# Cache pages laid four tokens to a partition, with evictions, page turns and key groups moved, in the sample loop of a decoder step

## The chip, the cores and the metric

The kernel runs as one program on one core of a Trainium2 chip. A core has five engines that follow their own instruction queues and meet through semaphores: PE (matmul and transpose), DVE (vector), ACT (scalar and activation), POOL and SP. In this kernel SP and POOL mostly issue DMAs, which the same 16 DMA engines carry out. The metric is device time of one execution, in microseconds (us), over three runs.

## The reference

One decoder layer is computed for a prompt of 256 tokens and a sample group of 8 sequences with 8 new tokens each. Every sample sequence has 1024 cached tokens, in 8 pages of 128 tokens that a page table names:

```
past = (gather_pages(cache_cmp_kv[l], page_table), gather_pages(cache_sel_kv[l], page_table), state_win_kv[l],
        gather_pages(cache_diff_k[l], page_table), gather_pages(cache_diff_v[l], page_table))
o_win  = local_attend(q_rot, win_all, pos, wpos)                    # last 512 tokens
o_cmp, p_cmp = compressed_attend(q_nsa, cmp_all, pos, ...)          # blocks of 32 tokens, stride 16
sel_idx = select_blocks(p_cmp, pos, tk)                             # 16 of 17 blocks of 64 tokens
o_sel  = selected_attend(q_rot, sel_all, sel_idx, pos)
o_nsa  = g0 * o_cmp + g1 * o_sel + g2 * o_win
o_diff = diff_attention(q_diff, k_all, v_all, pos, kpos, lam)       # softmax0 - lam * softmax1, then RMSNorm
x = x + (sig * (o_nsa @ w_br_nsa) + sig' * (o_diff @ w_br_diff)) @ w_out
x = x + moe_ffn(rmsnorm(x))                                         # top 4 of 32 experts
```

A softmax over cached keys and the sum over their values don't depend on the order in which the keys stand, so long as scores, masks and values have the same order. The change rests on this. The rows of the caches are 512 floats a token (difference keys, difference values) and 256 floats a token (selected, window and compressed K/V).

## The kernel before

The program runs in stages: input projection, prompt attention, the sample loop, the merge of the branches with the output projection, and the experts, whose weights (12 MB an expert, 32 experts and more blocks) stream in from the time at which the merge frees their places. The change is in the sample loop.

The loop handles two sequences a turn, in four turns; the last one is written out apart. All engines walk it in step, by counters. In a turn PE does this, in order:

- `dif_scores(0)`: the score products of the first sequence (L632) with the transposed keys `kdT`;
- 16 products of the compressed K hidden layer, `hidden(0, l)` (L587), with the transposes of the second sequence's key pages, groups `kd0` to `kd7` (L573), one after each odd `l`;
- `dif_scores(1)`, the compressed keys, 16 products `hidden(1, l)` with the groups `sel0` to `sel3`, `win0`, `win1` (cached keys transposed) and `pd0` to `pd2` (softmax weights transposed) between them;
- scores of the selected and window branch (L714 to L722), `dif_values(0)` and `dif_values(1)` (L648), then the groups `nk0`, `nk1` (key pages of the next turn's first sequence), `ps0`, `ps1`, `jo`, `pw`, `pm`, `nk2` to `nk5`;
- `nsa_values` (L662), `nk6`, `nk7` and `o` (both outputs transposed).

Each group of transposes goes to one of three PSUM banks in turn, so group n waits until group n-3 has been evicted. `LOOP_ENGINE` says whether ACT (L828) or DVE (L780 and on) evicts a group; each does its own in the order of its instruction list. A group of page keys is four 128x128 transposes of one page.

The buffers of the loop and who fills them:

- `dk_raw` (8 pages of keys, one set) by SP, `dk_pages` (L483): page by page, each as its group has been transposed. SP fills it twice a turn.
- `sel_raw`, `win_raw` by SP (L469, L474), after `nsa_values` of the turn before, in SP's order behind the key pages.
- `dv_raw` (values, two sets of 8 pages) by POOL, `values_in` (L510), after `dif_values`.
- `cmp_raw` (8 pages) by POOL, `cmp_pages` (L455), after DVE has turned the page before (STREAM_TRANSPOSE, `turn_pages`, L898). PE's `hidden(0, 0)` waits for all 16 turns of pages of its turn (`cmp_turned`).

At the top of a turn SP and POOL also read page numbers from the page table. A page stands with its 128 tokens on 128 partitions: one DMA of a key page writes 128 rows of 2 KB, one of a selected page 128 rows of 1 KB. The masks in the code follow that order: `oldw` for the first 8 window tokens, and the mask of the one dropped selection block (`dropm`, 14 candidates), which is added to columns 64 to 959 of the scores (L957).

After the loop, SP loads weights and stored gate values into freed places (`sync_merge`, helper line L251).

Of the kernel before, what the change touches and what calls it, by code (L numbers as in the profile page):

```python
# [17 lines left out]
ALU = mybir.AluOpType  # L18
# [4 lines left out]
D = 1024  # L23
# [7 lines left out]
NPAGE = PAST // PAGE  # L31
NPOOL = (5 * NB * NPAGE + 3) // 4
WIN = 512
# [24 lines left out]
def shape_constants():  # L58
# [27 lines left out]
    a["oldw"] = np.where(np.arange(NT)[None] > t[:, None], 0, NEG)  # L86
# [6 lines left out]
    a["blk"] = np.tile(np.arange(1, PAST // SB - 1), (128, 1))  # L93
# [54 lines left out]
def build(nc, io, const_a, at_a, const_b, at_b):  # L148
    ctx = ExitStack()
    with ctx:  # L150
# [16 lines left out]
        def bank(k, n=512, off=0):  # L167
# [6 lines left out]

        dv_raw = [[at(6144 + 512 * j, 512) for j in range(NPAGE)],
                  [at(34304 + 512 * j if j < NPAGE - 1 else 30720, 512) for j in range(NPAGE)]]
# [16 lines left out]
        winT, selT = at(31232, 2, WIN), at(32256, 2, PAST)  # L193
# [29 lines left out]
        pgs, mass, imp, dropm = alloc(NCC + 1), alloc(14, 4), alloc(14), alloc(14)  # L223
# [224 lines left out]

        def cmp_pages(eng, pages, i, b, these=range(NPAGE), first=False):
# [8 lines left out]
        def sync_attention(sp, early):  # L458
# [4 lines left out]
            def sel_pages(i, pages, first=False):  # L463
                if not first:
                    past(sp, l_pv, i * VALUES)
                for b in range(2):
                    for k in range(2):
                        for h in range(4):
                            sp.dma_start(sel_raw[:, b, 4 * k + h],  # L469
                                         sel_d[bass.ds(pages[b][4 * k + h], 1)].rearrange("a p n -> (a p) n")).then_inc(sel_in[2 * b + k], 16)  # L470

            def win_pages(i):
                for b in range(2):
                    sp.dma_start(win_raw[:, b], win_d[bass.ds(2 * i + b, 1)].rearrange("a (s p) n -> p (a s) n", p=128)).then_inc(win_in[b], 16)  # L474

            def dk_pages(i, b, pages, first=False):

                for pg, page in enumerate(pages):
                    if first and b:
                        past(sp, l_tp, pg + 1)  # L480
                    elif not first:
                        past(sp, l_tp, i * L_TP + (NPAGE - L_TP + group_at(f"nk{pg}" if b else f"kd{pg}") + 1))
                    sp.dma_start(dk_raw[:, pg], kd_d[bass.ds(page, 1)].rearrange("a p n -> (a p) n")).then_inc(dk_in[pg // 4], 16)  # L483
# [19 lines left out]
        def pool_attention(pool, st):  # L503
            vd_d = io["cache_diff_v"][0].rearrange("n p h e -> n p (h e)")

            def values_in(pages, i, b, first=False):
                for pg, page in enumerate(pages):
                    if pg == 0 and not first:
                        past(pool, l_pv, i * VALUES + ((PV_D1 if b else PV_D0) - VALUES))
                    pool.dma_start(dv_raw[b][pg], vd_d[bass.ds(page, 1)].rearrange("a p n -> (a p) n")).then_inc(dv_in[2 * b + pg // 4], 16)  # L510
# [49 lines left out]
        def pe_attention(pe):  # L560
# [30 lines left out]
            def turn(i, final):  # L591
# [49 lines left out]
                def dif_values(b):  # L641
                    for k in range(2):
                        pe.wait_ge(dv_in[2 * b + k], i * 64 + 64)
                    for j in range(NPAGE + 1):
                        for h in range(4):
                            out = pv_dif[b][32 * h:32 * h + 32]
                            if j < NPAGE:
                                nc.tensor.matmul(out, ptl[:, j, 32 * h:32 * h + 32], dv_raw[b][j][:, 128 * h:128 * h + 128], start=(j == 0), stop=False)  # L648
# [2006 lines left out]
```

## Time and profile before

| | us |
|---|---|
| runs of the kernel | 1458.56, 1460.26, 1460.40 (median 1460.26) |
| the profiled execution | 1461.19 |
| its span | 1459.5 |
| PE busy | 1389.9 (95%) |
| second and third turn of the loop (279.26 to 375.96) | 48.48 and 48.22 |

How to read it: the span is cut into stretches in which different things bind. Durations of single instructions are means over their group. "DMA share" is how much of the time of the 16 DMA engines the packets took; it can be over 1, since packets overlap. An instruction on PE can be idle for a wait while the engine's busy share still reads high. Landing times run from the issue of a DMA to its semaphore. Time that an engine waits matters only if it is the engine on which the others wait. The granted clock of TensorE was 0.993 over the span (the higher level, 2.4 GHz).

### The profile page before, as it was taken

The page shows a single profiled execution, that of the slowest core. Times are in us where ns is not written, and L with a number is a line of the kernel's source. Part 1 is how long each engine was busy: PE and PEld are TensorE (multiplying, and loading weights), DVE is VectorE, ACT ScalarE, POOL GpSimd, SP SyncE. Part 2 cuts the span into 40 slices and gives each one's busy share as a digit, 9 for nine tenths or more (in the row PEclk, how much of TensorE's full clock was granted, in tenths as well). Part 3 has the DMA queues.
Part 4 walks back from the last instruction along what each step waited for, and adds up shares of the span by engine and source line. Part 5 has one row for each costly group of instructions (what it writes and reads, how often), then busy time and mean ns, then how long its engine had stood idle before and what let it go on. Part 6 is the DMA issues. An engine that isn't in the chain of part 4 may idle for free.

```text
span 1459.5 us, 19997 instructions
## 1 busy us (share of the span) xinstructions
PE 1389.9 (95%) x7350; PEld 614.5 (42%) x7350; DVE 473.1 (32%) x1110; ACT 280.8 (19%) x584; POOL 106.1 (7%) x217
## 2 busy tenths in 40 slices
PE   7999998989999999999999999999999999999987
PEld 3446554766674454333333333333333333333322
DVE  1114474545633653132122221331331322213314
ACT  2003343444533121000101101101001001011002
POOL 1000223325400000000000000000000000000000
PEclk9999999999999999999999999999999999999999
DMA  7334686799988769999999999999999999999996
GB/s 264 115 115 169 245 174 219 192 302 279 300 261 241 298 252 428 427 428 430 427 428 430 428 428 428 429 428 428 428 429 427 428 430 427 428 430 428 428 427 256
DMA packets 92878, 509.45 MB, mean 349 GB/s; under 512 B 19066, under 2 KB 37986, under 8 KB 67586
## 3 DMA queue, kind: packets, MB, share of 16 engines
q1 hardware_dynamic: 77602, 480.99, 82.3%
q0 software_dynamic: 15232, 27.89, 6.6%
q8 instruction: 25, 0.41, 0.1%
q14 instruction: 19, 0.16, 0.0%
HBM read 502.25 MB, written 10.62 MB: 351 GB/s over the span
## 4 chain that ended last, share of the span: by engine, by line
PE 75%; DMA 19%; ACT 2%; issue 2%; SPq 1%; DVE 1%; ACTq 0%; DVEq 0%
PE PS L1435 25%; PE PS L1465 11%; DMA arena<-in_w_gate_up 10%; PE PS L1409 6%; PE PS L352 5%; DMA arena<-in_w_down 4%; PE PS L2129 4%; PE PS L1401 4%; PE PS L1116 2%; PE PS L1297 2%; DMA arena<-in_cache_sel_kv 2%; PE PS L587 2%; PE PS L573 2%; DMA arena<-in_cache_diff_k 2%; PE PS L361 1%
## 5 line engine op out<-in xcount | busy, mean ns | idle before, releaser
L1435 PE MATMUL PS<-arena 128*64 128x512 f32 x2048 | 456.2, 595 | 13.9 <-DMA arena<-in_w_gate_up 12.9
L1435 PEld LDWEIGHTS PS<-arena 128*64 128x64 f32 x2048 | 141.5, 137 | 295.2 <-issue 263.1
L1465 PE MATMUL PS<-arena 128*64 128x512 f32 x1024 | 226.9, 594 | 2.3 <-DMA arena<-in_w_down 2.2
L1891 DVE TENSOR_SCALAR arena<-PS 128x512 f32<-128x512 f32 x32 | 22.1, 692 | 451.1 <-PE PS L1444 450.1
L1465 PEld LDWEIGHTS PS<-arena 128*64 128x64 f32 x1024 | 71.8, 137 | 150.5 <-issue 144.3
L1409 PE MATMUL PS<-arena 128*128 128x512 f32 (+1 forms) x180 | 84.2, 608 | 0.0
L1401 PE MATMUL PS<-arena 128*128 128x512 f32 (+1 forms) x192 | 79.4, 617 | 4.5 <-ACT arena L1601 3.7
L1258 POOL COPY arena<-arena 96x64 bf16 (+1 forms) x34 | 8.1, 240 | 996.0 <-PE PS L1472 944.7
L352 PE MATMUL PS<-arena 128*128 128x512 f32 (+1 forms) x192 | 78.9, 572 | 1.6 <-DMA arena<-in_w_in 1.6
L573 PE MATMUL PS<-arena 128*128 128x128 f32 (+1 forms) x456 | 67.8, 281 | 12.1 <-DMA arena<-in_cache_diff_k 5.5
L1812 DVE TENSOR_TENSOR arena<-PS,arena 128x512 f32<-128x512 f32 x32 | 21.8, 688 | 163.7 <-PE PS L1417 161.2
L587 PE MATMUL PS<-arena 128*128 128x252 f32 x256 | 71.1, 392 | 3.8 <-DVE arena L898 3.8
L1586 ACT ACTIVATE arena<-arena 128x512 f32<-128x512 f32 x32 | 20.2, 630 | 269.7 <-DVE arena L1891 269.7
L1593 ACT ACTIVATE arena<-PS 128x512 f32<-128x512 f32 x32 | 19.1, 597 | 251.0 <-PE PS L1452 251.0
L573 PEld LDWEIGHTS PS<-arena 128*128 128x128 f32 (+1 forms) x456 | 53.6, 143 | 26.8 <-ACT arena L828 7.4
L1600 ACT ACTIVATE arena<-PS 64x512 f32<-64x512 f32 x31 | 18.3, 591 | 226.6 <-PE PS L1472 226.6
L2129 PE MATMUL PS<-arena 128*128 128x512 f32 x128 | 59.1, 603 | 0.6 <-ACT arena L2366 0.6
L828 ACT ACTIVATE arena<-PS 128x512 f32<-128x512 f32 (+2 forms) x75 | 40.9, 561 | 85.9 <-PE PS L573 78.8
L352 PEld LDWEIGHTS PS<-arena 128*128 128x128 f32 x192 | 37.0, 194 | 43.1 <-issue 41.6
L1409 PEld LDWEIGHTS PS<-arena 128*128 128x128 f32 (+1 forms) x180 | 31.6, 188 | 46.3 <-issue 46.3
L455 POOL DMA_DIRECT2D arena<-in_cache_cmp_kv x64 | 43.5, 687 | 79.2 <-DVE arena L898 78.9
L587 PEld LDWEIGHTS PS<-arena 128*128 128x128 f32 x256 | 43.8, 196 | 11.2 <-DVE arena L898 7.5
(293 smaller groups left out, 1279.4 us busy)
## 6 DMA issues: line engine op xcount, KB each, us to landing
arena<-in_w_gate_up SPq DMA_DIRECT2D x128, 2048.0 KB, 20.1
arena<-in_w_down SPq DMA_DIRECT2D x62, 2048.0 KB, 22.2
arena<-in_w_in SPq DMA_DIRECT2D x9, 2048.0 KB, 12.6
arena<-in_cache_diff_k SPq DMA_DIRECT2D x64, 256.0 KB, 6.8
arena<-in_cache_diff_v POOLq DMA_DIRECT2D x64, 256.0 KB, 8.7
arena<-in_cache_cmp_kv POOLq DMA_DIRECT2D x64, 128.0 KB, 5.6
arena<-in_cache_sel_kv SPq DMA_DIRECT2D x64, 128.0 KB, 7.9
arena<-in_state_win_kv SPq DMA_DIRECT2D x8, 512.0 KB, 8.6
```

The lines of the kernel that those rows point to most:

```text
L352: last = nc.tensor.matmul(bank(proj_bank(q, 2 * s + t))[:, 0:w], xnT[:, k, 128 * t:128 * t + 128], chunk_at(j)[:, k, 0:w], start=(k == 0), ...
L455: eng.dma_start(cmp_raw[:, pg], cmp_d[bass.ds(pages[pg], 1)].rearrange("a (k r) n -> (a r) k n", r=4)).then_inc(cmp_in[pg // 4], 16)
L573: last = nc.tensor.transpose(place[0:c, col:col + r], src, ident[0:r, 0:r])
L587: last = nc.tensor.matmul(hidden_at[c], w1[:, c, l, :], cmp_window(c, l), start=(l == 0), stop=(l == CB // 2 - 1))
L828: copy = lambda d, s: nc.scalar.activation(d, s, ACT.Copy)
L1116: last = nc.tensor.matmul(bank(BRANCH_BANK[v][half])[p:p + r], src[:, k, 128 * t:128 * t + r], w[:, k, 512 * nh:512 * nh + 512], start=(k ...
L1297: last = nc.tensor.matmul(bank(Z_BANK[v])[p:p + r], mT[:, k, 128 * t:128 * t + r], w_out[:, k, 512 * nh:512 * nh + 512], start=(k == 0), s ...
L1401: last = nc.tensor.matmul(out, spread[:, 128 * t:128 * t + ROWS[t]], ypair[:, 512 * h:512 * h + 512], start=True, stop=True)
L1409: last = nc.tensor.matmul(bank(h), pick[0:ROWS[t], t], hn[t][0:ROWS[t], 512 * h:512 * h + 512], start=(t == 0), stop=(t == 2))
L1435: last = nc.tensor.matmul(bank(2 + role + 2 * u)[64 * h:64 * h + 64], hTm[:, k, BS * u:BS * u + BS], gu_w[:, k, D * role + 512 * h:D * rol ...
L1465: last = nc.tensor.matmul(bank(6 + u)[64 * h:64 * h + 64], aT[u][:, c % 4, 64 * (c // 4):64 * (c // 4) + 64], down_w[u][c // 4][:, c % 4, ...
L2129: last = nc.tensor.matmul(bank(7), xnT[:, k, 128 * t:128 * t + 128], chunk_at(j)[:, k], start=(k == 0), stop=(k == KD - 1))
```

## The change

- **Page layout.** A key, value, selected or window row on a partition becomes four consecutive tokens. A page DMA now writes 32 partitions with 8 KB each (keys, values) or 4 KB each (selected): page `pg` goes to partitions 32 * (pg % 4) and on, columns of quad `pg // 4`. Four pages together fill a 128-partition quad. The window DMA still writes 128 partitions, with one piece of 4 KB in place of four of 1 KB. The compressed pages stay as they are.
- **Release of key pages.** Since every transposed group now reads all four pages of a quad, SP waits once for four groups (`kd3`, `kd7`, `nk3`, `nk7`), and then issues four DMAs.
- **Masks.** The token order within 512 scores is now (4, 128); `oldw` and the mask of the dropped block follow it. The latter is two DVE instructions over 512 columns instead of one over 896.
- **Places.** `dv_raw[1]` is one piece at 33792, `winT` and `selT` move down by 512 columns, so `winT` shares columns with the second gate staging area, and its eviction waits for the last gate store (`gates_stored(eng, 11)`).
- **Key groups on PE.** `kd0` to `kd6` stand after `hidden` 0, 2, ... 12 and `kd7` after 13, so that two products follow it.
- **Evictions on ACT.** `nk2` and `nk3` are evicted before the table load for the square root, not behind the root.
- **Page turns on DVE.** The last four turns of pages stood behind the eviction of `o`. Two now stand before the wait for `nsa_values`, two between the last output sum and that eviction. The output sum is three instructions, not four.
- **Gate loads.** After the loop `gates1` is loaded before `gates2`, and no longer waits for `dif_values(1)`.

```diff
+        def in_runs(raw, quad, h):
+            rows = PAGE // RUN
+            return raw[rows * h:rows * h + rows, RUN * quad:RUN * quad + RUN, :]
+        def page_runs(pool_d, page):
+            return pool_d[bass.ds(page, 1)].rearrange("a (p r) n -> (a p) r n", r=RUN)
...
-                            sp.dma_start(sel_raw[:, b, 4 * k + h],
-                                         sel_d[bass.ds(pages[b][4 * k + h], 1)].rearrange("a p n -> (a p) n")).then_inc(sel_in[2 * b + k], 16)
+                            sp.dma_start(in_runs(sel_raw[:, b], k, h), page_runs(sel_d, pages[b][4 * k + h])).then_inc(sel_in[2 * b + k], 16)
...
-                    sp.dma_start(win_raw[:, b], win_d[bass.ds(2 * i + b, 1)].rearrange("a (s p) n -> p (a s) n", p=128)).then_inc(win_in[b], 16)
+                    sp.dma_start(win_raw[:, b], win_d[bass.ds(2 * i + b, 1)].rearrange("a (p r) n -> (a p) r n", r=RUN)).then_inc(win_in[b], 16)
...
                 for pg, page in enumerate(pages):
-                    if first and b:
-                        past(sp, l_tp, pg + 1)
-                    elif not first:
-                        past(sp, l_tp, i * L_TP + (NPAGE - L_TP + group_at(f"nk{pg}" if b else f"kd{pg}") + 1))
-                    sp.dma_start(dk_raw[:, pg], kd_d[bass.ds(page, 1)].rearrange("a p n -> (a p) n")).then_inc(dk_in[pg // 4], 16)
+                    if pg % RUN == 0:
+                        if first and b:
+                            past(sp, l_tp, pg + RUN)
+                        elif not first:
+                            past(sp, l_tp, i * L_TP + (NPAGE - L_TP + group_at(f"nk{pg + RUN - 1}" if b else f"kd{pg + RUN - 1}") + 1))
+                    sp.dma_start(in_runs(dk_raw, pg // RUN, pg % RUN), page_runs(kd_d, page)).then_inc(dk_in[pg // 4], 16)
...
-                    pool.dma_start(dv_raw[b][pg], vd_d[bass.ds(page, 1)].rearrange("a p n -> (a p) n")).then_inc(dv_in[2 * b + pg // 4], 16)
+                    pool.dma_start(in_runs(dv_raw[b], pg // RUN, pg % RUN), page_runs(vd_d, page)).then_inc(dv_in[2 * b + pg // 4], 16)
...
+                keys_behind = {0: 0, 2: 1, 4: 2, 6: 3, 8: 4, 10: 5, 12: 6, 13: 7}
                 for l in range(CB // 2):
                     hidden(0, l)
-                    if l % 2:
-                        group(f"kd{l // 2}")
+                    if l in keys_behind:
+                        group(f"kd{keys_behind[l]}")
...
                 st(nc.scalar.activation(sqj, osq, ACT.Square, accum_out=lsum[:, 5:6]), l_sq)
+                ev("nk2", "nk3")
                 table(ACT.Sqrt, 2)
                 act.wait_ge(l_var, i + 1)
                 st(nc.scalar.activation(lvar, lvar, ACT.Sqrt), l_root)
-                ev("nk2", "nk3", "nk5", "nk6", "nk7")
+                ev("nk5", "nk6", "nk7")
...
-                mid = s_old[:, SB:SB + n14 * SB].rearrange("p (a b) -> p a b", b=SB)
-                st(V.tensor_tensor(mid, mid, dropm.unsqueeze(2).to_broadcast([128, n14, SB]), ALU.add))
+                drop = dropm.rearrange("p (q b) -> p q b", q=2)
+                for q in range(2):
+                    quad = s_old[:, 512 * q:512 * q + 512].rearrange("p (r b n) -> p r b n", r=RUN, n=SB // RUN)
+                    st(V.tensor_tensor(quad, quad, drop[:, q].unsqueeze(1).unsqueeze(3).to_broadcast([128, RUN, 8, SB // RUN]), ALU.add))
...
                 ev("nk4")
+                if not final:
+                    turn_pages(i + 1, 1, pages=(4, 5))
                 past(dve, l_pv, i * VALUES + PV_NSA)
...
-                st(V.scalar_tensor_tensor(osm[:, 0:64], pv_nsa[:, 2], lcf[:, 0:1], osm[:, 0:64], ALU.mult, ALU.add))
-                st.own()
-                st(V.tensor_copy(osm[:, 64:128], osm[:, 0:64]), l_osm)
+                st(V.scalar_tensor_tensor(osm.rearrange("p (a d) -> p a d", a=2), pv_nsa[:, 2].unsqueeze(1).to_broadcast([128, 2, 64]), lcf[:, 0:1],
+                                          onrm[:, 0:64].unsqueeze(1).to_broadcast([128, 2, 64]), ALU.mult, ALU.add), l_osm)
+                if not final:
+                    turn_pages(i + 1, 1, pages=(6, 7))
                 ev("o")
-                if not final:
-                    turn_pages(i + 1, 1, pages=range(4, NPAGE))
...
-            load(sp, "gates2", gsig[0:ROWS[2], 2], gate_pre[0:ROWS[2], 4 * D:6 * D])
-            past(sp, l_pv, PAIRS_OF_SEQ * VALUES + (PV_D1 - VALUES))
-            load(sp, "gates1", gsig[0:ROWS[1], 1], gate_pre[0:ROWS[1], 2 * D:4 * D])
+            for t in (1, 2):
+                load(sp, f"gates{t}", gsig[0:ROWS[t], t], gate_pre[0:ROWS[t], 2 * D * t:2 * D * t + 2 * D])
```

On SP, in the loop, the key pages (L483 before, L493 now; the REGISTER_ALU rows prepare a wait) stand so before:

```order
L388 ISA
L483 ISA
L483 DMA arena<-in_cache_diff_k 128x512
L388 REGISTER_ALU
L483 ISA
L483 DMA arena<-in_cache_diff_k 128x512
L388 REGISTER_ALU
L483 ISA
L483 DMA arena<-in_cache_diff_k 128x512
```

and so now:

```order
L389 REGISTER_ALU
L493 ISA
L493 DMA arena<-in_cache_diff_k 32x2048
L493 ISA
L493 DMA arena<-in_cache_diff_k 32x2048
L493 ISA
L493 DMA arena<-in_cache_diff_k 32x2048
L493 ISA
L493 DMA arena<-in_cache_diff_k 32x2048
L389 REGISTER_ALU
```

A wait before each page became one before four, and the shape went from 128 partitions with 512 floats to 32 partitions with 2048 floats, in one contiguous run.

On PE, the end of the first 16 hidden products (L587, two rows of MATMUL for two products) with key groups (L573), up to `dif_scores(1)` (L632), before:

```order
L587 MATMUL PS<-arena 128x252 x2
L388 REGISTER_ALU
L573 MATMUL PS<-arena 128x128 x4
L587 MATMUL PS<-arena 128x252 x2
L388 REGISTER_ALU
L573 MATMUL PS<-arena 128x128 x4
L388 REGISTER_ALU x2
L632 MATMUL PS<-arena 32x512 x8
```

and now (L597, L583, L642):

```order
L597 MATMUL PS<-arena 128x252 x2
L389 REGISTER_ALU
L583 MATMUL PS<-arena 128x128 x4
L597 MATMUL PS<-arena 128x252
L389 REGISTER_ALU
L583 MATMUL PS<-arena 128x128 x4
L597 MATMUL PS<-arena 128x252 x2
L389 REGISTER_ALU x2
L642 MATMUL PS<-arena 32x512 x8
```

Two hidden products now stand between the last key group and the scores that wait for its eviction.

On DVE, from the eviction of `nk4` (L780) over the output sum (L991 to L997) and the eviction of `o` (L807) to the page turns (L898), before, with the rows of L132 and L388 and three of the four rows of L807 left out:

```order
L780 COPY arena<-PS 128x4x128
...
L991 TENSOR_SCALAR arena<-PS,arena 128x64
...
L993 SCALAR_TENSOR_TENSOR arena<-PS,arena 128x64
...
L995 SCALAR_TENSOR_TENSOR arena<-PS,arena 128x64
...
L997 COPY arena<-arena 128x64
...
L807 COPY arena<-PS 64x4x8
...
L810 TENSOR_SCALAR arena<-PS,arena 128x4x16
L898 STREAM_TRANSPOSE arena<-arena 128x8x8x4 x4
```

and now (L791, L911, L1009 to L1013, L819, L822):

```order
L791 COPY arena<-PS 128x4x128
L911 STREAM_TRANSPOSE arena<-arena 128x8x8x4 x2
L1009 TENSOR_SCALAR arena<-PS,arena 128x64
...
L1011 SCALAR_TENSOR_TENSOR arena<-PS,arena 128x64
...
L1013 SCALAR_TENSOR_TENSOR arena<-PS,arena 128x128
L911 STREAM_TRANSPOSE arena<-arena 128x8x8x4 x2
...
L819 COPY arena<-PS 64x4x8
```

Two page turns moved ahead of the sum and two behind it, all four ahead of the eviction of `o`, and the copy is gone.

## Rows read from the trace of the kernel before

**Rows 1.** Page: the span in 40 slices, and the costliest weight DMAs in it.
```profile
DMA  7334686799988769999999999999999999999996
GB/s 264 115 115 169 245 174 219 192 302 279 300 261 241 298 252 428 427 428 430 427 428 430 428 428 428 429 428 428 428 429 427 428 430 427 428 430 428 428 427 256
```
**Rows 2.** Chain of waits in order of time: start us, us, what.
```profile
246.53 14.77 DMA arena<-in_cache_diff_k
...
303.45 16.07 DMA arena<-in_cache_sel_kv
...
351.47 16.26 DMA arena<-in_cache_sel_kv
...
395.35 11.87 DMA arena<-in_cache_diff_k
...
852.19 23.50 DMA arena<-in_w_gate_up
```
**Rows 3.** Who waited for whom on PE, 327.74 to 375.96 (one turn).
```profile
PE PS L573 <- ACT arena L828: 1.2, 1, 1.2
PE PS L587 <- DVE arena L898: 0.8, 1, 0.8
PE PS L632 <- DVE arena L780: 0.8, 1, 0.8
PE PS L573 <- DMA arena<-in_cache_sel_kv: 0.6, 1, 0.6
PE PS L573 <- DVE arena L997: 0.4, 1, 0.4
PE PS L632 <- issue: 0.3, 1, 0.3
```
**Rows 4.** Timeline, DVE, 343.2 to 350.8: start us, us, line, shapes, [idle before].
```profile
343.44 0.14 DVE L986 RECIPROCAL arena<-arena 128x1 f32<-128x1 f32 x1
343.63 0.29 DVE L988 TENSOR_SCALAR arena<-arena 128x128 f32<-128x128 f32 x1
343.84 0.68 DVE L780 COPY arena<-PS 128x512 f32<-128x512 f32 x1
345.86 0.28 DVE L991 TENSOR_SCALAR arena<-PS,arena 128x64 f32<-128x64 f32 x1 [1.34 <-PE PS L669]
...
346.82 0.20 DVE L997 COPY arena<-arena 128x64 f32<-128x64 f32 x1
...
348.73 1.98 DVE L898 STREAM_TRANSPOSE arena<-arena 128x256 f32<-128x256 f32 x4
```
**Rows 5.** DMAs issued 327.74 to 375.96: queue, count, KB each, median us to landing.
```profile
arena<-in_cache_diff_k SPq DMA_DIRECT2D x17, 256.0 KB, 5.5
arena<-in_cache_diff_v POOLq DMA_DIRECT2D x16, 256.0 KB, 8.9
arena<-in_cache_cmp_kv POOLq DMA_DIRECT2D x16, 128.0 KB, 5.5
arena<-in_cache_sel_kv SPq DMA_DIRECT2D x16, 128.0 KB, 10.6
arena<-in_state_win_kv SPq DMA_DIRECT2D x2, 512.0 KB, 8.9
```
**Rows 6.** Stretches: us, busy of PE, PEld, DVE, ACT, POOL, clock, DMA share, GB/s.
```profile
327.74:375.96 48.22, 43.88 (x531) 32.58 (x531) 27.08 (x84) 22.41 (x43) 20.46 (x35) 1.00 0.95 283
391.00:403.00 12.00, 10.31 (x175) 7.47 (x176) 6.24 (x19) 4.34 (x8) 2.67 (x5) 1.00 1.04 389
407.00:412.00 5.00, 4.74 (x21) 4.16 (x22) 0.69 (x1) 0.60 (x1) 0.00 (x0) 0.66 1.10 347
416.00:420.00 4.00, 4.00 (x45) 3.09 (x38) 2.00 (x4) 2.02 (x4) 0.00 (x0) 1.00 1.04 216
421.00:424.00 3.00, 3.00 (x21) 2.65 (x20) 2.03 (x8) 1.04 (x4) 0.00 (x0) 1.00 1.04 425
465.00:469.00 4.00, 4.00 (x12) 1.85 (x11) 1.81 (x3) 0.60 (x1) 0.00 (x0) 1.00 1.00 216
```
**Rows 7.** Timeline, SP's queue, 412 to 464: start us, us, line, what.
```profile
413.03 1.39 SPq L251 DMA_DIRECT2D arena<-in_w_br_nsa  x2
414.47 1.07 SPq L251 DMA_DIRECT2D arena<-in_w_br_diff  x2
...
460.28 0.43 SPq L251 DMA_DIRECT2D arena<-in_b_gate_up  x1
...
462.62 0.42 SPq L251 DMA_DIRECT2D arena<-in_b_down  x1
```
**Rows 8.** DMAs issued 462.6 to 462.9, the last of the bias pieces.
```profile
arena<-in_b_down SPq DMA_DIRECT2D x1, 128.0 KB, 7.4
```

## What the change will do to the time

> **What bounds the kernel now.** I read the slices of the page first [rows 1]: from the sixteenth slice, about 550 us, to the end the DMA engines move 427 to 430 GB/s with no gap. These are the expert weights, and the chain of waits runs through them again and again (its first such piece is at 852.19 [rows 2]). Their start is tied to the merge, and the merge to the end of the sample loop. So a microsecond won or lost in the loop is one at the end; nothing behind the loop absorbs it. The change is inside the loop, whose full turns last 48.22 us [rows 6].
>
> In a turn two things are close to each other. PE is busy for 43.88 of 48.22 us, and the view of waits gives the rest [rows 3]: 1.2 us before an `nk` group for an eviction by ACT, 0.8 for the page turns of DVE, 0.8 for the eviction of `kd7`, 0.6 for selected pages, 0.4 for the output sum, 0.3 of issue. The DMA share in the same stretch is 0.95 at 283 GB/s [rows 6]. And the chain of waits goes through DMAs in every turn: a selected page at 303.45 and 351.47, key pages at 246.53 and 395.35 [rows 2]. So the loop is bound by PE with a DMA side that is nearly full; whichever is made longer wins.
>
> **What the small steps give.** The ACT step takes away the 1.2 us: `nk5` no longer waits behind the table load and the root. What is late next is the output sum: DVE ends `nk4` at 344.52, the next two turns of pages cost half of 1.98 us, so 345.5, and three instructions of some 0.35 us with their own waits end at about 346.6 to 346.8, where the copy ended at 347.02 (346.82 + 0.20) [rows 4]. The root comes 1.1 us later than before, just as DVE gets to L986 at 343.44, so it adds next to nothing. Group `o` starts 0.3 to 0.5 us earlier; I take 0.4. The other 1.2 us are idle before `o` now. The page turns end before the eviction of `o`, so the wait of 0.8 us before `hidden(0, 0)` goes whole. `kd7` gets two hidden products as cover, about 0.86 us by the spacing of the products, against a wait of 0.8 us: gone too. Sum 0.4 + 0.8 + 0.8 = 2.0 us a turn, and 0.6 more if the selected pages land in time: a PE-bound turn of 46.2 to 45.6 us. The second mask instruction costs DVE some 0.2 us, while PE has `dif_values` before it; it would show in `ps0` only beyond about 1 us. The waits on the gate stores are long past, and the gate loads are awaited after the loop by ACT only; both nothing, or 0.3 us if PE has no other cover.
>
> **What the page layout costs.** A turn moves [rows 5] 16 key pages and 16 value pages of 256 KB, 16 selected pages of 128 KB (17 key issues fall in the window, 16 belong to a turn), 16 compressed pages of 128 KB and two windows of 512 KB: 13312 KB or 13.63 MB, which agrees with 283 GB/s over 48.22 us. Of these 10240 KB, 10.49 MB, will now be written to 32 partitions at a time.
>
> What do they run at now? Key and value pages, 2 KB a partition on 128 partitions: 389 GB/s with full engines. Selected and window pages, 1 KB: 347 GB/s [rows 6]. So at 0.95 of 48.22 = 45.8 us of DMA time, keys and values (8.39 MB) take 21.6, selected 6.0, windows 3.0, and 15 us are left for the compressed pages.
>
> What will they run at? The trace has transfers of exactly the new shapes: the bias loads into 32 partitions, 2048 floats (256 KB) and 1024 floats (128 KB). The first is issued at 460.28 and the last at 462.62, which lands 7.4 us later, at 470.0 [rows 7, 8]; between 465 and 469 the rate is 216 GB/s with a share of 1.00 [rows 6]. The two loads of `w_br_nsa`, each into one half of the partitions, give 216 GB/s too, at a share of 1.04, and the loads with 128 partitions right behind them 425 [rows 6, 7]. So it isn't the piece size: 4 KB and 8 KB pieces go at half rate when they reach 32 or 64 partitions, and the second DMA, into the other half, doesn't run beside the first. One queue of quarter pages gets 216 GB/s, little more than half of the 389 of now.
>
> The Trainium skill has a rule for this, in SBUF — State Buffer, section Door 1: The DMA port swizzle: partitions 0 to 31 reach 8 of 16 ports, with 189 GB/s measured at 1 MiB. By this rule, the trace agrees: the rate halves where only one half of the partitions is written. A rule for the change is in DMA: Bandwidth & Descriptors, Rules for kernel authors, which wants many small transfers made into few large ones; by that alone the turn would be PE-bound.
>
> Unknown is what SP's queue and POOL's queue do together, one on the lower and one on the upper half. Bounds: no gain, 216 GB/s, 48.6 us a turn for the 10.49 MB; full overlap, 428 GB/s, 24.5 us. Half of the time both would be on the same half, a fifth of the bytes (6.3 MB of SP against 4.2 of POOL) has no partner, and rows 6 show no gain between the halves within a queue; the row that it is nearest to is 216. I take 250 GB/s: 42 us. Add the windows, 1.05 MB at 425 = 2.5 us, and for the compressed pages between 0 (they fill what the halves leave free) and 15 us; I take 7.5. Together 52 us of DMA a turn. It is above the 46 us of PE, so the DMA sets the turn: 52.0 - 48.2 = +3.8 us. The whole loop loads 46080 KB, 3.46 turns' worth: +13 us. The gathered release adds to it: page 4 of the keys is now asked for when `nk7` is done, with three others behind one another; three pages at 216 GB/s are 3.6 us, against a gap of some 9 us to `kd4`, which already was late once (11.87 us in the last turn [rows 2]). I put 2 us on it for the whole loop, from 0 to 8. Sum: 1461.19 + 15 = 1476. The profiled execution is 0.9 us over the median of the runs, so I predict 1475.
>
> Where it shows first: `kd0`, `kd4` and the last `sel` and `win` groups wait for their pages. SP's queue brings keys and selected pages in one line, and values of POOL take turns with them.
>
> **The rivals.**
>
> *The two queues complement each other, PE stays the bound.* If the combined rate stays over 275 GB/s (10.49 MB in 48.2 - 2.5 - 7.5 = 38.2 us), the DMA no longer loses time, and over about 300 the turn is PE's. Then each of four turns gives 2.6 us, and the first and last give their key waits partly back: -10 to -12, 1449 to 1451. For it: POOL and SP are both busy in the crowded stretch from 344 to 371, values are loaded with 20 us to spare, and the compressed pages could fill idle ports. Against it: 216 GB/s with full engines on one queue.
>
> *Nothing overlaps.* If a pair of DMAs on different halves gains nothing, the turn is 48.6 + 2.5 + 7.5 = 58.6 us or, with the compressed pages at their full 15 us, 66: +10.4 x 3.46 = +36 at least by the first, 1497. The Trainium skill says so, in SBUF — State Buffer, section "Can I just issue two DMAs to hit both halves?": +6% for two concurrent DMAs. By that figure the estimate is 229 GB/s, 55.8 us a turn, +26 us. No row here has two queues on different halves.
>
> *It evens out.* DMA and PE both at 47 to 49 us: 1457 to 1463. For it: only that the two bounds lie so close.
>
> *The change isn't what it says*: if the pieces were still 2 KB, the half rate would stay, since it hangs on the partitions. This changes no number.
>
> **How the numbers follow.** Forecast (partial overlap, 1464 to 1483) 0.38; nothing overlaps (1484 to 1505) 0.22; PE stays the bound (1448 to 1457) 0.32; even (1457 to 1463) 0.08. The range 1449 to 1497 leaves out about 0.1 above and less below; within the forecast's own case it is 1464 to 1483. Faster or slower counts from 0.2%, 2.9 us, about what a measurement of this kernel can tell from no change: faster 0.32, within 0.08, slower 0.60.
>
> **What would show it.** In the profile after: full turns of 50 to 55 us in place of 48.2; a DMA share near 1 through the loop with a lower GB/s than 283; PE waits for key, selected or window DMAs of several microseconds a turn, and landing times of key pages over 8 us. The waits for L828, L898 and L780 of 1.2, 0.8 and 0.8 us gone, and one for the output sum of 1 to 1.5 us in place of 0.4. I am wrong if stretches of the loop with quarter pages alone move over 300 GB/s; then the turns are about 46 us and the kernel is faster. I am also wrong if the stretch behind the loop changes its length by more than 1 us: then the time at the end doesn't follow the loop.

## The result, and the profile after

The changed kernel took 1511.87 us, median of four runs (1508.17 to 1515.89), against 1460.33 for the kernel before (1458.56 to 1463.02): a ratio of 1.036, 95% interval 1.0331 to 1.0388. It is slower by 52 us. I had forecast slower, but by 15 us, with a range that ended at 1497. The profiled execution took 1515.25 us, 54.1 over that of before; its span is 1513.5 us.

The page of the changed kernel: the span in 40 slices, TensorE's clock in tenths, the DMA share in tenths, GB/s.

```profile
PEclk9999998999879999999999999999999999999999
DMA  7336758999999667999999999999999999999996
GB/s 254 111 111 195 242 135 209 197 217 204 222 218 261 197 287 293 428 427 428 428 428 429 428 429 429 428 428 429 428 429 428 429 428 428 429 429 429 428 428 257
```

Beside [rows 1] the weight stream at 428 GB/s starts one slice later and is otherwise the same. The slices of the sample loop from the eighth to the thirteenth have their engines full (9 in the row DMA) and move 197 to 261 GB/s.

The loop's turns, from one `dif_scores(0)` to the next: us, busy of PE, PEld, DVE, ACT, POOL, clock, DMA share, GB/s.

```profile
248.04:305.85 57.81, 45.96 (x530) 34.53 (x531) 29.32 (x86) 22.60 (x44) 22.54 (x40) 0.91 0.94 204
305.85:369.46 63.61, 48.25 (x531) 35.87 (x531) 27.11 (x83) 22.69 (x43) 20.79 (x37) 0.92 1.04 209
369.46:439.40 69.94, 50.25 (x534) 38.07 (x535) 26.67 (x82) 22.02 (x41) 19.44 (x37) 0.83 1.04 212
```

Between the same marks the kernel before had, for its full turns:

```profile
299.58:348.03 48.45, 43.97 (x530) 32.56 (x531) 27.07 (x83) 22.39 (x43) 20.50 (x35) 1.00 0.95 282
348.03:395.97 47.94, 43.89 (x531) 32.62 (x532) 26.97 (x82) 22.12 (x43) 22.13 (x39) 1.00 0.96 284
```

A full turn was 48.45 and 47.94 us at 282 and 284 GB/s. It is 63.6 and 69.9 us now, at 209 and 212 GB/s with a share of 1.04: the same bytes at three quarters of the rate.

Who waited for whom on PE in the second turn (305.85 to 369.46), by groups of instructions: busy us, mean ns, idle before.

```profile
L583 PE MATMUL PS<-arena 128*128 128x128 f32 (+1 forms) x114 | 18.4, 297 | 13.5 <-DMA arena<-in_cache_diff_k 6.6 <-DMA arena<-in_state_win_kv 5.1 <-DVE arena L1013 1.5
```

And over the last four turns and what follows (240 to 600): us in total, times, longest.

```profile
PE PS L583 <- DMA arena<-in_cache_diff_k: 29.9, 5, 8.9
PE PS L658 <- DMA arena<-in_cache_diff_v: 9.4, 2, 7.9
PE PS L583 <- DMA arena<-in_state_win_kv: 8.2, 4, 3.9
PE PS L1133 <- DMA arena<-in_w_br_diff: 4.3, 1, 4.3
PE PS L583 <- DVE arena L1013: 4.0, 3, 1.5
```

The waits of [rows 3] for the ACT eviction and for `kd7` are gone or small, as forecast, and the wait for the output sum went from 0.4 us to between 1.3 and 1.5, as forecast. In their place stand 47.5 us for pages of keys, values and windows, against 6.8 in the same view of the kernel before.

The DMAs issued in the second turn: queue, count, KB each, median us to landing.

```profile
arena<-in_cache_diff_k SPq DMA_DIRECT2D x17, 256.0 KB, 16.8
arena<-in_cache_diff_v POOLq DMA_DIRECT2D x16, 256.0 KB, 25.2
arena<-in_cache_cmp_kv POOLq DMA_DIRECT2D x18, 128.0 KB, 20.5
arena<-in_cache_sel_kv SPq DMA_DIRECT2D x16, 128.0 KB, 16.5
arena<-in_state_win_kv SPq DMA_DIRECT2D x2, 512.0 KB, 25.6
```

Against [rows 5]: key pages 16.8 us for 5.5, values 25.2 for 8.9, and the compressed pages, which weren't changed at all, 20.5 for 5.5. They share the DMA engines with the rest.

From one `dif_scores(0)` to the next, and then to the first product of the merge after group `o` (450.75 before, 503.19 now), the kernel lost 5.0, 15.2, 22.0 and 9.0 us, and 1.3 ahead of the first: 52.4 of 54.1. In the last stretch 4.8 us are the longer wait for keys (6.9 for 2.05) and 2.9 the wait for `w_br_diff` (4.3 for 1.35), queued behind it; and the eight products after that wait took 5.87 us instead of 3.70. The granted clock from 490 to 496 is 0.62, a mean of the higher and the lower level.

### The profile page after: what moved, and what is told of

Read it like the earlier page. It is cut to its first block, busy times and chain, and to the rows that moved or that the text cites. A ratio compares the mean times of both kernels' runs of the same rounds, so it can differ in the third digit from the quotient of the medians.

```text
span 1513.5 us, 19966 instructions
## 1 busy us (share of the span) xinstructions
PE 1406.2 (93%) x7350; PEld 624.5 (41%) x7350; DVE 473.1 (31%) x1110; ACT 280.8 (19%) x584; POOL 102.3 (7%) x217
## 4 chain that ended last, share of the span: by engine, by line
PE 69%; DMA 24%; issue 2%; SPq 2%; DVE 2%; ACT 1%; POOL 0%; POOLq 0%; DVEq 0%; ACTq 0%
PE PS L1451 24%; PE PS L1481 11%; DMA arena<-in_w_gate_up 9%; PE PS L1425 5%; PE PS L353 5%; DMA arena<-in_w_down 4%; PE PS L2145 4%; PE PS L1417 3%; DMA arena<-in_cache_diff_v 3%; DMA arena<-in_cache_diff_k 2%; PE PS L1313 2%; DMA arena<-in_state_win_kv 2%; PE PS L583 2%; PE PS L597 2%; PE PS L362 1%
## 5 line engine op out<-in xcount | busy, mean ns | idle before, releaser
L583 PE MATMUL PS<-arena 128*128 128x128 f32 (+1 forms) x456 | 72.3, 294 | 42.7 <-DMA arena<-in_cache_diff_k 29.9
L583 PEld LDWEIGHTS PS<-arena 128*128 128x128 f32 (+1 forms) x456 | 57.8, 151 | 58.6 <-issue 36.5
L597 PE MATMUL PS<-arena 128*128 128x252 f32 x256 | 78.2, 421 | 1.2 <-DVE arena L911 1.2
L353 PEld LDWEIGHTS PS<-arena 128*128 128x128 f32 x192 | 37.2, 195 | 44.5 <-issue 43.0
L597 PEld LDWEIGHTS PS<-arena 128*128 128x128 f32 x256 | 47.7, 214 | 9.0 <-issue 3.4
L1425 PEld LDWEIGHTS PS<-arena 128*128 128x128 f32 (+1 forms) x180 | 31.6, 188 | 46.3 <-issue 46.3
```

Source lines behind the costliest of these rows:

```text
L353: last = nc.tensor.matmul(bank(proj_bank(q, 2 * s + t))[:, 0:w], xnT[:, k, 128 * t:128 * t + 128], chunk_at(j)[:, k, 0:w], start=(k == 0), ...
L583: last = nc.tensor.transpose(place[0:c, col:col + r], src, ident[0:r, 0:r])
L597: last = nc.tensor.matmul(hidden_at[c], w1[:, c, l, :], cmp_window(c, l), start=(l == 0), stop=(l == CB // 2 - 1))
L1425: last = nc.tensor.matmul(bank(h), pick[0:ROWS[t], t], hn[t][0:ROWS[t], 512 * h:512 * h + 512], start=(t == 0), stop=(t == 2))
```

## The experiments

Each ran beside the kernel before on the same chip; the median of the kernel before was 1460.0 to 1460.5. Three of the kernels were run once only, and the text says so.

**steps_only.** The old layout with all the steps:

```diff
-                    sp.dma_start(in_runs(dk_raw, pg // RUN, pg % RUN), page_runs(kd_d, page))...
+                    sp.dma_start(dk_raw[:, pg], kd_d[bass.ds(page, 1)].rearrange("a p n -> (a p) n"))...
```
(so too for values, selected pages and windows, with the old masks and a wait per key page)

> The changed kernel with the old page layout (128 partitions a page, a wait per key page), so only the moved evictions, page turns, key groups, the shorter output sum and the gate loads are left of the change. My theory (the whole loss is the rate of pages that reach a quarter of the partitions, and the steps are a gain that the DMA hides): full turns of 45.6 to 46.4 us in place of 48.2, waits for L828, L898 and L780 gone, 7 to 10 us under the kernel before, 1450 to 1453. Rival (the steps take part in the loss, since key groups are now needed half a step earlier and page turns delay the output sum): turns of 48 us or more, 1460 or more.

Measured: 1461.95 us, ratio 1.0008 (0.9991 to 1.0025). No gain. Its waits on PE from 240 to 440:

```profile
PE PS L582 <- DMA arena<-in_cache_diff_k: 9.2, 5, 3.1
PE PS L582 <- DVE arena L1009: 3.8, 3, 1.3
PE PS L582 <- DMA arena<-in_cache_sel_kv: 3.7, 3, 1.8
```

The three waits that the steps remove are gone, but those for keys and selected pages grew from 6.8 us (5.5 and 1.3) to 12.9, and the full turns are 50.3 and 48.9 us. So my theory fell here: I had 7 to 10 us for the steps. As I read it, the loop before was bound by PE and its DMAs at once, and only the first was relieved; the runs with later values below look at what the DMAs lost.

**layout_only.** The changed kernel without the moved evictions, page turns and key groups; the output sum in three instructions and the new order of the gate loads stay:

```diff
-                keys_behind = {0: 0, 2: 1, 4: 2, 6: 3, 8: 4, 10: 5, 12: 6, 13: 7}
+                (kd pages after each odd l; nk2, nk3 behind the root; four page turns behind the eviction of o)
```

> The changed kernel with the steps on PE, ACT and DVE taken back, so the layout, the gathered release and the masks are left. My theory: DMA sets the turn, so the steps don't matter: full turns of 60 to 70 us at 205 to 215 GB/s, the same time as the changed kernel within 4 us (1506 to 1518). Rival (the steps are part of the loss): clearly faster than the changed kernel, 1500 or less; rival (steps still pay): 1520 or more.

Measured: 1502.91 us (1502.29 to 1509.29), ratio 1.0307 (1.0273 to 1.0341); full turns of 62.2 and 68.3 us at 209 and 215 GB/s. That is just under the 1506 to 1518 that I had expected. The layout, with its masks and its release in fours, is 42 of the 52 us by the medians, 45 by the ratio. With the layout the steps cost 8 to 9 us more, though the same mechanism sets the turn; the value and compressed loads that DVE's earlier page turns release come earlier then. I did not separate that cost further.

**spread_pages.** The same pieces, other partitions. The mask of the dropped block follows the new order (not shown), with two DVE instructions more:

```diff
-            return raw[rows * h:rows * h + rows, RUN * quad:RUN * quad + RUN, :]
+            return raw[h:128:RUN, RUN * quad:RUN * quad + RUN, :]
```

> The changed kernel with the same pieces of 8 and 4 KB, the same 32 partitions a page and the same gathered release, but page h goes to every fourth partition (h, h + 4, ...) in place of a block of 32; the mask of the dropped block follows with two DVE instructions more a turn. Theory 1 (what counts is which part of the partitions a DMA reaches): keys and values at 380 GB/s or more, full turns of 45.6 to 46.5 us, 1447 to 1454. Theory 2 (it is the number of partitions, 32, or two big pieces for each DMA engine, or the release in fours): turns of over 55 us, 1495 or more.

Measured: 1454.8 us (1452.5 to 1459.34), ratio 0.9964 (0.9948 to 0.998). That is 57 us under the changed kernel by one subscript and its mask, with the pieces of 8 and 4 KB, the number of 32 partitions and the release in fours all kept. It is just over the 1447 to 1454 of the first theory, and 40 us under the second. Its full turns:

```profile
299.50:346.81 47.31, 43.60 (x531) 32.58 (x531) 27.03 (x85) 22.29 (x43) 20.05 (x36) 1.00 0.89 287
346.81:393.60 46.79, 43.80 (x534) 32.54 (x535) 26.83 (x84) 22.15 (x42) 21.31 (x39) 1.00 0.92 301
```

The DMA share is 0.89 and 0.92 at a higher rate than before, and in the first of these turns ten finer slices in a row, of 1.2 us each, move 395 to 436 GB/s. What matters is which partitions a DMA reaches: a block of 32 is slow, 32 spread over all 128 is as fast as all. The Trainium skill says in SBUF — State Buffer, section Door 1: The DMA port swizzle, that bits 4 to 2 and bit 6 of the partition number choose the port; by that rule every fourth partition reaches all 16 ports. The run agrees.

**alternate_halves.** The changed kernel with another order of the pages in each queue:

```diff
-                for pg, page in enumerate(pages):
+                for pg in (0, 2, 1, 3, 4, 6, 5, 7):
```

> The changed kernel with the pages of each quad issued in the order 0, 2, 1, 3 by SP and POOL, so that neighbours in a queue are on different halves of the partitions. If nothing overlaps between halves (what the changed kernel's 204 to 212 GB/s with both queues full suggests): full turns of 60 to 70 us as in the changed kernel, 1505 to 1518. If DMAs on different halves can run beside each other when they stand next to each other: over 250 GB/s in the full stretches, turns under 56 us, under 1490.

Measured, run once: 1491.7 us. Its turns:

```profile
304.11:361.60 57.49, 47.43 (x531) 35.89 (x531) 26.94 (x83) 22.46 (x43) 19.67 (x36) 0.91 1.04 235
361.60:419.40 57.80, 49.56 (x530) 36.53 (x531) 26.69 (x82) 22.11 (x42) 20.59 (x39) 0.88 1.04 239
```

Between the two expectations: neighbours on different halves gain something, 235 to 239 GB/s in place of 209 to 212, but far from the 428 of full overlap.

**opposite_halves.** The changed kernel, POOL's values in another order than SP's keys:

```diff
-                for pg, page in enumerate(pages):
+                for pg in (2, 3, 0, 1, 6, 7, 4, 5):      # values only
```

> The changed kernel, with POOL issuing the value pages of a quad in the order 2, 3, 0, 1, while SP keeps 0, 1, 2, 3, so that the queues begin on opposite halves of the partitions. If two queues on opposite halves run beside each other: over 240 GB/s in the full stretches and turns of 56 to 60 us as with pages of alternating halves, near 1492. If it needs neighbours in one queue (or the two queues don't stay opposite): 200 to 218 GB/s, turns of 62 to 70 us, 1505 to 1518.

Measured, run once: 1510.3 us, full turns of

```profile
305.63:368.20 62.57, 48.27 (x530) 35.99 (x531) 26.93 (x83) 22.57 (x43) 19.67 (x36) 0.89 1.04 213
368.20:432.07 63.87, 49.40 (x530) 37.69 (x531) 26.63 (x82) 22.15 (x42) 20.59 (x39) 0.87 1.04 222
```

213 and 222 GB/s, 2% and 5% over the changed kernel; the time is that of the changed kernel. So the order of one queue against the other gives next to nothing. Whether the queues ever stood on opposite halves for long can't be seen in these traces. These rates hold windows and compressed pages too; few_compressed gives the rate of the quarter pages by themselves.

**few_compressed.** The changed kernel with the compressed pages of the second to fourth pair cut to 16 rows of 256 bytes. The rest of these pages is not loaded, and PE computes on what lay there before:

```diff
+                    eng.dma_start(cmp_raw[0:16, pg, 0:64], cmp_d[bass.ds(pages[pg], 1), 0:16, 0:64].rearrange("a p n -> (a p) n"))...
```

> The changed kernel, with the compressed pages of the second to fourth pair cut to 16 rows of 256 bytes a page, so 2.10 MB a turn less. It tells whether these pages fill what the half rate leaves free. If they are hidden (I took half): turns stay over 60 us, 1505 or more. If they add to the quarter pages in full, 10 to 15 us a turn: turns of 49 to 54 us, 1470 to 1482.

Measured, run once: 1488.0 us; the full turns, and stretches in them:

```profile
303.11:358.85 55.74, 46.97 (x531) 35.04 (x531) 26.99 (x83) 22.53 (x43) 16.43 (x35) 0.94 0.93 209
358.85:413.25 54.40, 46.91 (x531) 35.06 (x532) 26.66 (x81) 22.20 (x42) 17.42 (x37) 0.94 0.95 211
303.11:330.00 26.89, 20.44 (x138) 14.25 (x138) 5.75 (x12) 6.56 (x12) 4.90 (x10) 0.94 1.03 220
358.85:386.00 27.15, 20.96 (x140) 14.60 (x141) 6.39 (x15) 6.94 (x14) 4.90 (x10) 0.93 1.03 218
344.00:348.00 4.00, 4.00 (x128) 3.41 (x120) 3.83 (x10) 0.97 (x1) 3.37 (x10) 1.00 0.04 8
```

The turns are 7.9 and 15.5 us shorter than in the changed kernel. That is less than a full effect (I had expected 49 to 54 us and 1470 to 1482 for it), and far from none. The third and fourth rows give the number for which I had no row: in them SP's queue (3.8 of the 5.9 MB) and POOL's queue (2.1) move keys, selected pages and values into quarters, both queues at once and the engines full, with almost no compressed pages. The rate is 220 and 218 GB/s, 1 to 2% over the 216 of one queue. The last row shows why the turn doesn't fall further: there the engines have next to nothing to move, which the changed kernel's turns don't have. So 2.1 MB of compressed pages are not hidden in the slow quarter pages. The stretches of the changed kernel in which they run beside values show the same:

```profile
356.00:360.00 4.00, 3.96 (x87) 3.54 (x88) 1.93 (x6) 2.06 (x6) 3.58 (x8) 1.00 1.07 133
420.00:424.00 4.00, 0.00 (x0) 0.00 (x0) 0.00 (x0) 0.00 (x0) 2.47 (x6) 0.50 1.07 129
```

**gathered_release.** The kernel before, SP waiting once for four key groups:

```diff
-                    elif not first:
-                        past(sp, l_tp, ... group_at(f"nk{pg}" if b else f"kd{pg}") + 1))
+                    if pg % RUN == 0: past(sp, l_tp, ... group_at(f"nk{pg + RUN - 1}" if b else f"kd{pg + RUN - 1}") + 1))
```

> The kernel before, in which only SP's wait is changed: one wait for four key groups (kd3, kd7, nk3, nk7), then four page DMAs, with the old layout. I had put 2 us (0 to 8) on it for the loop. Theory (a small cost, since landing is set by the last page of the four in both): 1460 to 1463. Rival (the burst of four collides with values and selected pages): 1464 or more.

Measured: 1462.29 us, ratio 1.0016 (1.0002 to 1.0031): about 2 us, the value that I had put on it. This is the cost with the old layout; what the release in fours costs with contiguous quarter pages was not run.

**spread_no_steps.** spread_pages without the steps on PE, ACT and DVE (the edit of layout_only on top of that of spread_pages).

> The kernel with pages spread over every fourth partition, with the steps on PE, ACT and DVE taken back. With the kernel before (1460.5), steps_only (1462.0) and spread_pages (1454.8) it fills the square of layout and steps. Theory 1 (the loop before is bound by its DMAs, so the steps alone give nothing, and it takes the faster pages to let them show): the layout alone gives little too, since PE's waits for L828, L898 and L780 stay: turns of about 48 us, 1457 to 1461. Theory 2 (the larger pieces are the whole gain): as spread_pages, 1453 to 1456.

Measured: 1456.62 us (1452.73 to 1460.26), ratio 0.9974 (0.9957 to 0.9991). PE's waits from 240 to 440:

```profile
PE PS L641 <- DVE arena L789: 4.6, 5, 1.4
PE PS L582 <- ACT arena L838: 4.6, 6, 1.2
PE PS L596 <- DVE arena L908: 3.7, 4, 1.2
PE PS L582 <- DMA arena<-in_cache_diff_k: 2.9, 1, 2.9
PE PS L1129 <- DMA arena<-in_w_br_diff: 0.9, 1, 0.9
```

The full turns are 47.4 and 46.5 us, and the time lies between the two theories. Now no key page is waited for after the first turn, and the waits of the engines are all there. The layout alone is worth 0.3%; the steps on top of it 1.8 us more by the medians, which the intervals (0.9948 to 0.998 beside 0.9957 to 0.9991) don't tell from none. The square of four kernels: 1460, 1462 with the steps, 1457 with the spread pages, 1455 with both.

**steps_values_later** and **spread_values_later.** steps_only and spread_pages, in which POOL issues the second set of value pages of a turn only when the selected pages have landed:

```diff
+                pool.wait_ge(sel_in[3], (i + 1) * 64)
                 values_in(pages[1], i, 1)
```

> steps_only (old layout), and POOL issues the second set of value pages only when the selected pages have landed. steps_only came out at 1462.0, since waits of 1.5 us for key pages and 1.6 to 2.1 for selected pages took the place of those removed. Theory A (they come from value loads issued 3 us earlier, beside them): the waits go, 1452 to 1456. Theory B (the old layout's DMA time is simply full): DMA waits stay in another place, 1458 or more.

> spread_pages, and POOL issues the second set of value pages of a turn only when the selected pages of that turn have landed. Theory (the earlier page turns let POOL's value loads run into the key and selected pages, on which PE waits 1.2 to 1.5 us a turn in spread_pages): these waits go, turns of about 45.5 us, 1449 to 1453. Rival (the values are then late for the second value products, or the crowd only moves): 1455 or more.

Measured: 1456.98 us, ratio 0.9983 (0.9965 to 1.0), and 1458.6 us, ratio 0.998 (0.9966 to 0.9994). In the old layout the full turns are 46.8 and 46.0 us, together the shortest of all kernels here, where steps_only had 50.3 and 48.9:

```profile
300.12:346.93 46.81, 44.83 (x530) 33.09 (x531) 26.65 (x82) 22.30 (x43) 19.08 (x34) 0.96 1.01 282
346.93:392.89 45.96, 43.17 (x530) 32.76 (x531) 26.44 (x81) 22.08 (x42) 17.89 (x32) 1.00 1.06 291
```

In steps_only POOL issued the eight value pages of this set at 349.73, 2.1 us into its turn; in the kernel before it was at 352.69, 4.7 us in. So the value loads that the steps brought forward, beside key and selected pages, took at least a part of the steps' gain, by these profiles. How much is open: the kernel before with only the values held back was not run, and by the intervals steps_values_later and steps_only just touch.

The time follows only in part, for two reasons. In its profiled execution the keys of the first turn came 6.1 us late, where steps_only waited 2.5. Such a wait ahead of the loop's first full turn, 2.2 to 6.1 us in the profiles of the kernels with the old layout, blurs differences of 2 to 3 us. And in the last turn the values held back run beside the weights of the merge. The rows show PE's eight products there, with start, us and the wait ahead of them, in steps_only and steps_values_later, then in spread_pages and spread_values_later:

```profile
439.13 3.70 PE L1129 MATMUL PS<-arena 128*128 128x512 f32 x8 [0.99 <-DMA arena<-in_w_br_diff]
434.48 6.66 PE L1130 MATMUL PS<-arena 128*128 128x512 f32 x8 [3.70 <-DMA arena<-in_w_br_diff]
432.54 3.70 PE L1133 MATMUL PS<-arena 128*128 128x512 f32 x8 [0.84 <-DMA arena<-in_w_br_diff]
437.38 6.55 PE L1134 MATMUL PS<-arena 128*128 128x512 f32 x8 [2.79 <-DMA arena<-in_w_br_diff]
```

The delay costs 5.7 and 4.8 us there. With the spread pages the full turns are 47.2 and 46.4 us, no longer than the 47.3 and 46.8 of spread_pages, and the fourth turn starts at the same time (393.58 and 393.57). The values are waited for, 4.0 us in all, of which 2.7 in the last turn, and that turn with its merge is what makes it slower than spread_pages by the medians (1458.6 to 1454.8). A delay that leaves out the last turn was not run.

**spread_sum_first.** spread_pages, with DVE's four page turns behind the output sum:

```diff
                 ev("nk4")
-                if not final:
-                    turn_pages(i + 1, 1, pages=(4, 5))
...
-                    turn_pages(i + 1, 1, pages=(6, 7))
+                    turn_pages(i + 1, 1, pages=(4, 5, 6, 7))
```

> spread_pages, with all four page turns of DVE behind the output sum instead of two ahead of it. PE waited 1.25 us for the sum before group o in every turn of spread_pages. Theory (the sum sets o, and the page turns still end before the next hidden products): the wait goes to 0.3 us, turns 0.9 us shorter, 2 to 4 us less than spread_pages, 1450 to 1453. Rival (the DMA binds and takes it back, as it did in steps_only): 1454 to 1457.

Measured: 1455.21 us (1452.61 to 1458.55), ratio 0.9963 (0.9948 to 0.9978); no better than spread_pages. From 296.43 to 391.53 its waits on PE are among others

```profile
PE PS L582 <- DMA arena<-in_cache_diff_k: 3.3, 2, 2.1
PE PS L582 <- DMA arena<-in_state_win_kv: 0.9, 1, 0.9
PE PS L582 <- ACT arena L839: 0.8, 2, 0.4
```

The wait before `o` fell from 1.25 to 0.4 us, and the keys gave it back. Both kernels, 5 us under the kernel before, are the best that I found.

## Why the prediction was too small

The side was right, and so was the mechanism (quarter pages at half rate let the DMAs set the turn). The size was wrong by a factor of 3.5. By its own steps:

- *The time at the end follows the loop.* Right: 52.4 of 54.1 us are in by the merge, 1.7 us come behind it. I had said that over 1 us behind the loop would make me wrong; it is over, by 0.7. Of the 1.7 us, 1.3 are in one place. The first 16 products of the experts took 5.40 us instead of 3.65, at a granted clock of 0.67 instead of 1.00, and the 16 ahead of them were 0.45 us faster. Their waits were the same in both kernels. spread_sum_first has 6.10 us there, so it isn't the slow layout; why the clock fell is open.
- *What the steps give, 2.0 us a turn.* The waits went as said, and the new one of about 1.3 us before `o` came as said. That they would also be worth it in a PE-bound loop was wrong: steps_only gave nothing. A step on DVE let POOL's loads start earlier, and by the run with later values these took a part of it from what PE needed next. I had treated the PE-bound turn of 46 us as a level that the DMAs of the old layout would allow.
- *A quarter page goes at 216 GB/s.* Right, from the bias loads [rows 7, 8], and shown to be the partitions by spread_pages. The rule on few large transfers, which the prediction cites against it, doesn't bear on the change: the number of DMAs and their sizes stayed as they were, and only the piece on a partition grew.
- *Two queues together: 250 GB/s.* This term failed. I had chosen it between 216 and 428 without a row, nearest to 216 but not at it. Measured are 218 and 220 (few_compressed). With 219 the 10.49 MB take 47.9 us a turn in place of 42.
- *The compressed pages, 7.5 of 0 to 15 us.* This term failed too, and by more. With 47.9 for the quarter pages and 2.5 for the windows, 16.4 of the mean full turn of 66.8 us are left for them, since the engines are full all the time. That is an estimate; 2.10 MB in 16.4 us are 128 GB/s, near the 129 and 133 of the two stretches above, which hold some values too. Taking most of them out shortened the turn by 7.9 and 15.5 us, and left the engines empty for a few us. So the sum of a turn was 52.0 and should have been 66.8: 5.9 us more for the rate of the two queues, and 8.9 more for the compressed pages. By 3.46 turns' worth of loads 66.8 would have been +64 us, measured +54, as the first and last turn lost less than the full ones.
- *The rival "nothing overlaps".* It was the true case, at its upper price. I had given it 0.22 with the times 1484 to 1505, so the measured time had no chance in any of the cases, and I had ended the range at this rival's lower price, 1497. I had worked the upper price out for a turn (66 us) and not carried it into the range. The estimate from the Trainium skill's +6% (SBUF — State Buffer, section "Can I just issue two DMAs to hit both halves?"), 229 GB/s and 55.8 us a turn, was nearer than mine. Its rate is 4 to 5% over the measured one, and the rest of what it lacks is the compressed pages. Where neighbours in a queue alternate between the halves, the rate of the whole turn rose by some 13% (alternate_halves).
- *The release in fours, 2 us.* gathered_release: 2 us in the old layout. The reason I gave, three quarter pages behind one another at 216 GB/s, is one of the new layout and was not tested by itself.
- *"PE stays the bound"*, 0.32, needed over 275 GB/s. That both queues were busy together and values had time to spare said nothing of the rate of quarter pages.

The clock has a part that I left out. In the changed kernel the granted clock is 0.83 to 0.92 over the turns, where it was 1.00. After PE has been idle 6 to 9 us for a page, its products run at the lower level (1.2 GHz) for some microseconds (granted clock 0.50 from 448.8 to 452): four transposes took 1.11 us in place of 0.65, the first 64 products of `dif_values(1)` 3.64 in place of 1.95. After shorter waits both were seen: four transposes took 0.65 us after 3.9 us idle and 1.11 after 2.7. PE was busy 50.25 us in the slowest turn against 43.88, with about the same instructions. How much of this is hidden while the DMAs set the turn was not measured. After the last waits it isn't hidden, as the 2.2 us on the first merge products show.

## What to carry to other kernels

Before a tile is laid out anew for larger DMA pieces, look at which partitions one DMA reaches: a transfer into a contiguous quarter or half of them went at about half the rate here, and the same pieces on every fourth partition did not. Find in the trace any transfer of the new shape and take its rate for the whole traffic, both queues together, until a row shows overlap. Carry the worse end of each unknown into the range. When an engine that isn't on the path is sped up, ask which loads its buffers release, and what these run into.

## What the runs showed of the hardware

- DMAs into 32 contiguous partitions with pieces of 8 and 4 KB: 218 and 220 GB/s from both queues together at a DMA share of 1.03 (few_compressed); into 32 partitions, every fourth one, up to 436 GB/s (spread_pages). The engines are full in both cases, and the share says nothing of the rate.
- The order of pages within a queue matters (alternating halves, 13% more, run once), the order of one queue against the other hardly did (2 and 5%, run once).
- Compressed pages from POOL's queue, beside values: 129 to 133 GB/s at a share of 1.07 (the changed kernel).
